# Token-major first stage with twelve places for modulation weights, and the gated branch sums on VectorE

## The reference

```
xs = x_sample + grid_pos_embed(rows)           # sin/cos of the row in channels 0:512, of the column in 512:1024
mod = silu(c) @ w_ada + b_ada                  # 6 x 1024 columns: shift1, scale1, gate1, shift2, scale2, gate2
h = rms_norm(x, g0) * (1 + scale1) + shift1
z = h @ w_in                                   # inputs of all mixers and the merge gates
y = (sig(gA) * A + sig(gB) * B + sig(gC) * C) @ w_out     # A Fourier, B pooling, C mLSTM, each projected
x = x + gate1 * rms_norm(y, g1)
x = x + gate2 * rms_norm(swiglu(rms_norm(x, g2) * (1 + scale2) + shift2), g3)
```

## Time and profile before

| | |
|---|---|
| median of three runs | 1853.43 us (1850.91 to 1862.03) |
| profiled execution | 1859.34 us |
| its span, first to last instruction | 1857.5 us |
| busy share TensorE / VectorE / ScalarE / GpSimd | 96 / 44 / 33 / 23% |
| transfers over the span | 296.19 MB, mean 159 GB/s |

### The profile page before, as it was taken

One profiled execution on the slowest core, in us unless ns is written; L12 is line 12 of the kernel. 1 busy time (PEld: TensorE's weight loads), 2 busy tenths in 40 slices (PEclk: granted clock), 3 DMA queues, 4 the chain that ended last, 5 costly groups with the idle time before them and its releaser, 6 DMA issues.

```text
span 1857.5 us, 24614 instructions
## 1 busy us (share of the span) xinstructions
PE 1783.0 (96%) x9794; PEld 1650.2 (89%) x9794; DVE 819.9 (44%) x1246; ACT 607.8 (33%) x1025; POOL 427.3 (23%) x481
## 2 busy tenths in 40 slices
PE   7799999999999999989989899999999999999997
PEld 4599998989999999988978799999999999888885
DVE  5500002241443434437768965444444443454543
ACT  2321112233222222223656482222222223343432
POOL 0300000323122233235335453222222210000000
PEclk9799999999999999999999999999999999999999
DMA  5544344665345566689768332222222226657572
GB/s 196 196 166 141 140 169 175 227 202 164 100 159 180 168 197 199 195 232 295 238 207 257 112 117 71 72 71 72 71 73 75 76 75 185 210 179 233 178 232 74
DMA packets 175386, 296.19 MB, mean 159 GB/s; under 512 B 11967, under 2 KB 122242, under 8 KB 175280
## 3 DMA queue, kind: packets, MB, share of 16 engines
q1 hardware_dynamic: 132016, 163.88, 27.4%
q0 software_dynamic: 27328, 90.73, 15.1%
q10 hardware_dynamic: 15936, 40.11, 6.4%
HBM read 231.57 MB, written 63.10 MB: 159 GB/s over the span
## 4 chain that ended last, share of the span: by engine, by line
PE 82%; DVE 7%; DMA 3%; ACT 3%; POOL 2%; issue 2%; ACTq 0%; DVEq 0%; SPq 0%; POOLq 0%
PE bank L532 25%; PE bank L534 25%; PE bank L533 25%; DVE w_lo L1652 2%; PE bank L722 1%; DMA mg<-z_scratch 1%; PE bank L751 1%; PE bank L954 1%; PE bank L957 1%; PE bank L964 1%; PE bank L972 1%; DMA raw<-in_w_ada 1%; POOL ya L2410 1%; DVE h_lo L2197 1%; DVE mg L1990 1%
## 5 line engine op out<-in xcount | busy, mean ns | idle before, releaser
L1652 DVE TENSOR_TENSOR w_lo<-raw,w_hi 128x1024 fp32r<-128x1024 f32 x218 | 283.8, 1304 | 377.7 <-ACT w_hi L1207 377.1
L532 PE MATMUL bank<-h_hi,w_hi 128*128 128x384 f32 x1080 | 377.2, 349 | 8.1 <-DVE h_lo L2197 5.5
L533 PE MATMUL bank<-h_lo,w_hi 128*128 128x384 f32 x1080 | 367.4, 340 | 0.0
L534 PE MATMUL bank<-h_hi,w_lo 128*128 128x384 f32 x1080 | 367.3, 340 | 0.0
L1207 ACT CAST w_hi<-raw 128x1024 fp32r<-128x1024 f32 x218 | 226.2, 1049 | 281.6 <-PE bank L534 174.2
L532 PEld LDWEIGHTS bank<-h_hi,w_hi 128*128 128x128 f32 x1080 | 205.5, 190 | 24.5 <-ACT z_st L1251 10.1
L533 PEld LDWEIGHTS bank<-h_lo,w_hi 128*128 128x128 f32 x1080 | 205.5, 190 | 0.1
L534 PEld LDWEIGHTS bank<-h_hi,w_lo 128*128 128x128 f32 x1080 | 205.1, 190 | 0.0
L534 PE MATMUL bank<-w_hi,f_lo 128*128 128x512 f32 x396 | 158.0, 399 | 0.0
L533 PE MATMUL bank<-w_lo,f_hi 128*128 128x512 f32 x396 | 156.0, 394 | 0.0
L532 PE MATMUL bank<-w_hi,f_hi 128*128 128x512 f32 x396 | 155.2, 392 | 0.0
(11 more groups left out here) (310 smaller groups left out, 3212.3 us busy)
## 6 DMA issues: line engine op xcount, KB each, us to landing
raw<-in_w_stream SPq DMA_DIRECT2D x209, 512.0 KB, 4.6
z_scratch<-z_st ACTq DMA_DIRECT2D x44, 576.0 KB, 3.1
raw<-in_w_ada SPq DMA_DIRECT2D x48, 512.0 KB, 5.1
mg<-z_scratch ACTq DMA_DIRECT2D x24, 576.0 KB, 6.8
f_raw<-f_scratch SPq DMA_DIRECT2D x66, 192.0 KB, 4.2
zt<-z_scratch POOLq DMA_DIRECT2D x27, 256.0 KB, 3.8
raw<-in_k_dft SPq DMA_DIRECT2D x9, 512.0 KB, 3.7
kv_scratch<-kv_st POOLq DMA_DIRECT2D x9, 512.0 KB, 4.5
```

The source lines that it names most:

```text
L532: pe.matmul(out, a_hi, b_hi, start=start, stop=False)
L533: pe.matmul(out, a_hi, b_lo, start=False, stop=False)
L534: return pe.matmul(out, a_lo, b_hi, start=False, stop=stop)
L1652: dve.tensor_tensor(w_lo[:, slot], raw[:, slot], w_hi[:, slot].bitcast(F32), ALU.subtract).then_inc(s_wlo, 1)
```

## The change

Start: the position is added to x token-major, in `x_in` itself. The row half comes from two rows of a table that TensorE spreads over 128 tokens (`spread_row`, one matmul with `sel`), the column half from a 128 x 512 table. ScalarE squares a tile of 1024 and sums it in the same instruction, takes the root; VectorE scales the tile into `xr`; TensorE turns `xr`, and ScalarE copies the banks to `xn`. `x_mean`, `xT`, `sq` and `rstd1` are gone. The sixteen first `w_ada` units have twelve places, four of `raw` and eight of `ada_raw`, which lies where `w_hi` and `w_lo` will be; the loads of units 12 to 15 wait for units 1, 2, 3 and 5, the others for no unit. TensorE multiplies units between the x tiles. The sum with the position is stored to DRAM (`xp_dram`) by GpSimd after `h_full`, and `x_load` reads it from there. Merge: the two additions into `ya` stand in VectorE's list, behind `y_low` of the chunk before; `pos_load` and `pos_add` are gone. Two loads of constants move behind the first four z units.

```diff
@@ SP, start
-                if n >= RAW:
-                    sp.wait_ge(s_unit, n - RAW + 1)
-                load(n % RAW, w_ada[n:n + 1])
-            sp.dma_start(cst[:, CB_EARLY:], k_cst[:, CB_EARLY:CB["pool"].start]).then_inc(s_const, 16)
-            sp.dma_start(cst_p[:], k_cst[:, CB["pool"].start:]).then_inc(s_const, 16)
+                place, landed, _ = ada_slot(n)
+                if RAW <= n < 3 * RAW:
+                    sp.wait_ge(s_xin[n - RAW], 16)
+                if n == ADA_FIRST - 1:
+                    sp.wait_ge(s_unit, RAW + 2)
+                elif n >= 3 * RAW:
+                    sp.wait_ge(s_unit, n - 3 * RAW + 2)
+                sp.dma_start(place, w_ada[n]).then_inc(landed, 16)
+                if n == ADA_FIRST - 3:
+                    sp.wait_ge(s_unit, 1)
+                    for half in range(2):
+                        r = slice(512 * half, 512 * half + 512)
+                        sp.dma_start(raw[:, 0, r], w_stream[0, :, r]).then_inc(s_raw[0], 16)
...
             z1_turn(0, True)
+            sp.dma_start(cst[:, CB_EARLY:], k_cst[:, CB_EARLY:CB["pool"].start]).then_inc(s_const, 16)
+            sp.dma_start(cst_p[:], k_cst[:, CB["pool"].start:]).then_inc(s_const, 16)
@@ TensorE, start
+            def spread_row(c):
...
+                pe.matmul(bank[7][:, :], sel[:].rearrange("r a w -> r (a w)"), pos_row[:, c, :], start=True,
+                          stop=True).then_inc(s_prow, 1)
             def start():
+                spread_row(0)
+                spread_row(1)
+                n = 0
                 for c in range(NT):
+                    if c + 2 < LAT // P:
+                        spread_row(c + 2)
                     x_tile(c)
                     if c == 4:
-                        x_mean(0)
-                    elif c == 7:
-                        x_mean(1)
-                pe.wait_ge(s_cpad, 1)
-                pe.wait_ge(s_early, 16)
-                for n in range(ADA_FIRST):
-                    blk = n // ADA_G
-                    ada_unit(n, n, n % ADA_G, blk % 2, blk - 1 if blk >= 2 else None)
-                    if n == 1:
-                        x_mean(2)
-                    if n % ADA_G == 1 and n > ADA_G:
-                        ada_turn(n // ADA_G - 1, (n // ADA_G - 1) % 2)
+                        pe.wait_ge(s_cpad, 1)
+                        pe.wait_ge(s_early, 16)
+                    for _ in range(2 if c >= 5 else int(c == 4)):
+                        ada_first(n)
+                        n += 1
+                for n in range(n, ADA_FIRST):
+                    ada_first(n)
                 ada_turn(ADA_FIRST // ADA_G - 1, 1)
@@ ScalarE, start
+                for c in range(NT):
...
+                    act.activation(x_sq[:], x_in[:, c], ACT.Square, accum_out=stat[:, c, 0:1]).then_inc(s_xsq, 1)
...
+                    act.activation(stat[:, c, 1:2], stat[:, c, 0:1], ACT.Sqrt, bias=eps[:, 0:1],
+                                   scale=1.0 / D).then_inc(s_xsq, 1)
+                    if c:
+                        x_out(c - 1)
+                x_out(NT - 1)
                 for blk in range(ADA_FIRST // ADA_G):
+                    if blk == ADA_FIRST // ADA_G - 1:
+                        split(ADA_FIRST, ADA_FIRST)
                     ada_out(blk, ADA_G * blk + ADA_G - 1)
@@ VectorE, start
+            def add_pos(c):
...
+                dve.tensor_tensor(x_in[:, c, 0:h], x_in[:, c, 0:h], bank[7][:, :], ALU.add).then_inc(s_padd, 1)
...
+                dve.tensor_tensor(x_in[:, c, h:D], x_in[:, c, h:D], pos_col[:], ALU.add).then_inc(s_padd, 1)
+            def x_norm(c):
...
+                dve.reciprocal(stat[:, c, 1:2], stat[:, c, 1:2]).then_inc(s_xrstd, 1)
...
+                dve.tensor_scalar(xr[:, c % 3], x_in[:, c], stat[:, c, 1:2], None, ALU.mult).then_inc(s_xr, 1)
             def start():
+                add_pos(0)
                 for c in range(NT):
+                    if c + 1 < LAT // P:
+                        add_pos(c + 1)
+                    x_norm(c)
+                split(ADA_FIRST, ADA_FIRST, 0)
+                dve.wait_ge(s_xn, 2 * NT)
                 modulation()
-                split(ADA_FIRST, ADA_FIRST, 0)
@@ VectorE, e1
                     if c:
                         y_low(x - 1)
+                    if x >= 2:
+                        dve.wait_ge(s_yl, x - 1)
+                    dve.wait_ge(s_ym, x + 1)
+                    dve.tensor_tensor(ya[:, x % 2], mg[x % MG][:, 0], mg[x % MG][:, 1], ALU.add).then_inc(s_ya, 1)
+                    dve.wait_ge(s_ya, 2 * x + 1)
+                    dve.tensor_tensor(ya[:, x % 2], ya[:, x % 2], mg[x % MG][:, 2], ALU.add).then_inc(s_ya, 1)
@@ GpSimd, after h_full
+            for c in range(NT):
+                pool.dma_start(xp_dram[c], x_in[:, c]).then_inc(s_xps, 16)
+            pool.wait_ge(s_xps, 16 * NT)
@@ GpSimd, e1 and e2
-                for c in range(KT):
...
-                    pool.tensor_tensor(ya[:, x % 2], mg[x % MG][:, 0], mg[x % MG][:, 1], ALU.add).then_inc(s_ya, 1)
...
-                    pool.tensor_tensor(ya[:, x % 2], ya[:, x % 2], mg[x % MG][:, 2], ALU.add).then_inc(s_ya, 1)
...
+                pool.dma_start(xt[:, m % 3], xp_dram[tile_at(position(m))]).then_inc(s_xl[m % 3], 16)
...
-                pos_load(3 * g)
-                for k in range(KT):
-                    if k in (2, 4, 6):
-                        m = 3 * g + k // 2 - 1
-                        pos_add(m)
-                        if k < 6:
-                            pos_load(m + 1)
-                    if g == NG - 1 and k == 2:
-                        combine(0)
+                if g == NG - 1:
+                    combine(0)
```

More of the change, by code:

```diff
@@ L98 @@
 FR = 6
+START_LOADS = (2, 3, 2, 2, 2, 2, 2, 2, 1)
 CHAIN = (1, 0, 2)
@@ L475, in kind_of @@
             return int(tile_at(q) == NT - 1)
-        def pos_adds(m):
-            return sum(not kind_of(position(i)) for i in range(m + 1))
         def product_done(j, i):
@@ L621, in z1_turn @@
                     n0 = ADA_FIRST + 3 * u
-                    sp.wait_ge(s_unit, i * 12 + (n0 - RAW + 1))
-                    load(n0 % RAW, w_stream[bass.ds(i * RAW + u, 1)])
+                    if not (first and u == 0):
+                        sp.wait_ge(s_unit, i * 12 + (n0 - RAW + 1))
+                        load(n0 % RAW, w_stream[bass.ds(i * RAW + u, 1)])
                     if first and u == 0:
@@ L714, in ada_unit @@
             def ada_unit(n, n0, part, b, before):
-                pe.wait_ge(s_raw[n0 % RAW], slot_count(n, n0))
+                if isinstance(n, int) and n < ADA_FIRST:
+                    src, landed, count = ada_slot(n)
+                    pe.wait_ge(landed, count)
+                else:
+                    src = raw[:, n0 % RAW]
+                    pe.wait_ge(s_raw[n0 % RAW], slot_count(n, n0))
                 if part == 0 and before is not None:
@@ L738, in x_tile, with ada_first @@
                 if c >= 2:
[L739 removed]
+                    pe.wait_ge(s_xn, 2 * (c - 1))
                 for k in range(KT):
[L741 removed]
+                    m = pe.transpose(bank[2 * u + k // 4][:, ktile(k % 4)], xr[:, c % 3, ktile(k)], ident)
                     if k % 4 == 3:
                         m.then_inc(s_xt, 1)
[L745 to L752 removed]
+            def ada_first(n):
+                blk = n // ADA_G
+                ada_unit(n, n, n % ADA_G, blk % 2, blk - 1 if blk >= 2 else None)
+                if n in (2 * ADA_G + 1, 2 * ADA_G + 2, 3 * ADA_G + 1):
+                    done = (2 * ADA_G + 1, 2 * ADA_G + 2, 3 * ADA_G + 1).index(n)
+                    ada_turn(done, done % 2)
@@ L1653, in split @@
                                   ALU.subtract).then_inc(s_wlo, 1)
-            def x_evac(c):
-                for half in range(2):
-                    dve.wait_ge(s_xt, 2 * c + half + 1)
-                    ps = bank[2 * (c % 2) + half][:, :].rearrange("p (k r w) -> p k r w", k=4, r=2)
-                    out = xT[:, 4 * half:4 * half + 4, c * P:(c + 1) * P].rearrange("p k (r w) -> p k r w", r=2)
-                    if half == 0:
-                        pos = last(K["pos_r"].rearrange("p (k r) -> p k r", k=4)[:, :, 2 * c:2 * c + 2], GRID_W)
-                    else:
-                        pos = K["pos_c"].rearrange("p (k w) -> p k w", k=4).unsqueeze(2).broadcast_to(
-                            (P, 4, 2, GRID_W))
-                    dve.tensor_tensor(out, ps, pos, ALU.add).then_inc(s_xev, 1)
             def gain(i):
```

165 lines of the change are left out of this document (70 added, 95 removed).

## The result

The changed kernel takes 1844.67 us (median of 7 runs, 1842.44 to 1849.04) against 1853.43 us: the ratio is 0.9948, with an interval of 0.993 to 0.9966. On a second chip it took 1842.62 us against 1855.62: 0.9929 (0.9911 to 0.9948). The gain is 9 to 13 us, not 28.5. The profiled execution of the changed kernel took 1845.1 us with a span of 1843.2, at its median; the one of the kernel before lay 6 us above its median, so the spans differ by more (14.3 us) than the medians.

The account below looks back on a forecast made before the run. The prediction took TensorE, busy 96% of the span, as the bound, with winnable idle time at the start and in the merge. Gains of 20 + 8.5 = 28.5 us from the median of 1853.43 gave 1825 us, range 1814 to 1840.

Parts of the forecast that it names:

- The bound and the places of the change: Whole kernel: TensorE, busy 96%, is the bound; time can be won at the start and in the merge.
- So ScalarE and VectorE share the pace at about 2.7 us a tile, TensorE needs 2.0 and is not the bound: Start, tile loop: pace of 2.7 us a tile, last root at 31.7 us; the start gives 20 us.
- sign of being wrong: Start, tile loop: the forecast is wrong if the loop takes over 3 us a tile.
- The rival of the low clock: New start: TensorE at 1.2 GHz doubles 7.5 + 1.0 us, adding 8.5 for 1834; chance 0.10.
- bound of about 41: Start, modulation weight transfers: even with a faster loop the end cannot come before about 41 us, bounding the gain at 25.
- `xt` is loaded from the scratch at the same place: Merge: reading `xt` from the scratch leaves its load where it was; no cost counted.
- merge's 8.5 us: Merge, `e1` and `e2`: sums on VectorE and no `pos_add` shrink TensorE's gaps, 8.5 us together.
- terms of the third `e1` and the last `e2`: Merge, late part: gains of 0.5 us in the third `e1` and 2.4 of 6.04 us in the last `e2`.
- The removed position loads and `pos_add` save TensorE nothing else: Merge: removing 8 x 512 KB of position loads and `pos_add` gives TensorE no further gain.
- The nine stores of x cost nothing: Second z unit's loads: stores of 9 x 512 KB, 11.5 us, fit in slack of 5 us; nothing counted.
- The merge gives nothing: Merge: VectorE in order, with ScalarE waits in its path, ends as late or 3 us later; 1833 to 1836, chance 0.11.
- The start gives half: Start: unit 8 onward still waits on a chain, so TensorE's gain halves; 1835, chance 0.05.

Follow-up runs that it names:

- pos_by_dma: Changed kernel with the row half of the position brought by a 128x512 transfer per tile instead of `spread_row` on TensorE; 1837.43 us, ratio 0.9893.
- four_places: Changed kernel with one more wait on SP that gives the sixteen modulation units their four places back; 1851.78 us, ratio 0.9985.
- late_pos: Changed kernel with the edits of late_loads and pos_by_dma together; 1833.63 us, ratio 0.9882.
- before_again: The kernel before, unaltered, run once more for a second trace; 1856.18 us, span 1854.4.
- after_again: The changed kernel, unaltered, run once more on the chip of its variants; 1842.62 us, ratio 0.9929.
- late_loads: Changed kernel with one more wait: GpSimd issues a group's x loads only when that group's sums are done; 1837.86 us, ratio 0.9901.
- adds_gpsimd: Changed kernel with the merge's sums back on GpSimd and the x loads behind them; 1840.54 us, ratio 0.9909.
- adds_pos: Changed kernel with sums back on GpSimd, x loads behind them, and the position's row half by transfer; 1836.57 us, ratio 0.9888.
- sums_late: Kernel before with the sums on VectorE, and GpSimd's x and position loads waiting for the group's sums; 1851.22 us, ratio 0.9971.
- sums_vector: Kernel before with only the merge's two sums per chunk moved from GpSimd to VectorE; 1860.47 us, ratio 1.0026.
- warm: Changed kernel with filler matmuls on TensorE: six before the first `spread_row`, two behind each of the first five tiles; 1836.18 us, ratio 0.9893.

## Why the prediction was wrong

**The bound and the places of the change: right.** Time was won at the start, and what was won there stayed won: 11.9 us at the first z matmul, and 11.0 at the place of the earlier trace rows (102.34 and 102.56 us before, 90.97 and 91.96 after), by the means of two traces each.

**"So ScalarE and VectorE share the pace at about 2.7 us a tile, TensorE needs 2.0 and is not the bound": the step that failed.** The rows used for it (5.43 us for `x_mean`, 1.07 for eight transposes) are those of full clock. In the changed kernel a tile is 2.07 + 1.97 us at the low clock less a small overlap, 3.9 us, back to back from 12.4 to 39 us. The first root was forecast at 11.3 and ended at 12.8 us; the last was forecast at 31.7 and ended at 42.5. That is 10.8 us late. That ScalarE comes next was right, with 2.33 us instead of 2.7: so much a tile takes where TensorE isn't in the way (pos_by_dma), and there the whole start gains 19 to 20 us, as forecast. The prediction's own sign of being wrong, a tile loop over 3 us, came true.

**The rival of the low clock was priced at the wrong place.** It was given 8.5 us, but for "7.5 + 1.0 us" of units and turns behind the tiles, and with a chance of 0.10, on the ground that "the tile loop leaves under 1 us". From 12.37 us on the loop left none at all, and the clock stayed low for 27 us of unbroken work. The units behind the tiles ran at full clock: from the start of the last tile's transposes (43.50 us) to the end of the last turn (55.5 us) it took 12.0 us, where the forecast had 13 (33.0 to 46.1). In the profile of before the sign was there: the first 40 transposes took 7.41 us, where five times 1.07 is 5.35. A single one took 421 ns until 9.8 us and 272 ns behind that, so the first part of them ran at the low clock, and I took the figure for full clock from a later row. So the start gave 12 and not 20. The time of that rival (1834) is still 11 us below the result, because the merge failed as well.

**The places carry most of the start: right.** four_places takes 9.2 us back. But the transfers were forecast without a break to about 38 us, and they rest from about 32 to 40 us (0 GB/s from 36 to 40, above): units 12 to 15 wait on SP for units 1, 2, 3 and 5, which were forecast for 27 to 32 us and of which unit 1 was multiplied only from 37.62 us on. It cost nothing here, since TensorE waited for none of them. In late_pos the weights do set the end: the last lands at 45.5 us. The prediction's bound of about 41 is not tested by that, as late_pos carries 2 MB more, 5 us at 409 GB/s.

**"`xt` is loaded from the scratch at the same place": wrong, and the merge's 8.5 us with it.** The code is at the same place, the time isn't. GpSimd's list is in order, and its sums had held the loads back. I gave no thought to what an engine does earlier when work is taken from it. That VectorE keeps up with TensorE's 4.27 us a chunk holds (it needs 3.93 us, 844.66 - 840.73, where nothing holds it up, and 4.2 were counted), `w_lo` at 1.22 holds, and "no gap above 1 us in the first `e1`" fails with a stop of 3.09 us behind a `raw` that landed late.

The terms can be told apart when the merge's stretch of the table is split at the matmul behind the stop of 2.55 us (937.34 us before, 928.00 in the changed kernel):

| kernel | up to there | from there |
|---|---|---|
| before, before_again | 106.0, 103.7 | 106.3, 106.1 |
| changed, after_again | 108.7, 109.3 | 102.5, 102.8 |
| late_loads, late_pos | 105.7, 105.4 | 102.4, 102.5 |
| adds_gpsimd, adds_pos | 104.4, 106.4 | 103.9, 104.1 |
| sums_late | 102.5 | 104.7 |

From there on 0.5 + 2.4 = 2.9 us were forecast and 3.6 came, 2.2 of them without the sums on VectorE (adds_gpsimd, adds_pos). So the terms of the third `e1` and the last `e2` hold together, although the last `e2` still stops for 5.23 us, where 6.04 - 2.4 = 3.6 was forecast; the `w_lo` in front of that stop takes 2.28 us beside `combine`, not 1.22. Up to there 3.2 + 2.4 = 5.6 us were forecast, and 4.2 were lost. The early loads are 3 to 4 of that (changed against late_loads), and 9 in sums_vector against sums_late (111.4 and 102.5). But with late loads this part still gave between a loss of 0.7 (late_loads, late_pos) and a gain of 2.3 (sums_late), so the two terms were too high besides; single traces scatter by 2 to 3 us here. One stop that was to go even grew: the one of 2.55 us is 3.12 to 3.14 us in all nine traces with the sums on VectorE, and 2.55 or 2.56 in the four with the sums on GpSimd. The prediction had named ScalarE's stalls there as something that would "now delay the sums as well"; that they are the cause is not shown.

**"The removed position loads and `pos_add` save TensorE nothing else": wrong by 1 to 2 us.** All kernels without them have 811.6 to 812.8 us in the last column, all kernels with them 813.8 or 813.9. One stop behind the last `e2` shrank from 2.82 to 1.17 us:

```profile
1063.81 0.41 PE L530 MATMUL bank<-T_hi,S_hi 128*128 128x384 f32 x1 [1.17 <-DVE S_lo L2084]
```

No run takes them out alone, so that they are the cause is argued from this split only.

**The nine stores of x cost nothing: right in the changed kernel.** ScalarE waits longer for a weight than before (10.63 us for the one at 88.36, where the earlier trace rows had 6.52), so the loads do come later beside the stores, but TensorE has no stop there: the 5 us of slack that the prediction found covered it. No run leaves the stores out, so that they are the reason for the longer wait is argued.

```profile
88.36 1.05 ACT L1242 CAST w_hi<-raw 128x1024 fp32r<-128x1024 f32 x1 [10.63 <-DMA raw<-in_w_stream]
```

**The other rivals.** "The merge gives nothing" came true in size, for a reason that it did not name (loads, not ScalarE in VectorE's way, are most of it). "The start gives half" came close in size, 12 of 20 us, also for another reason than it named. Each alone would have stayed in the range; together they left it, and I had not added them.

## What to carry to other kernels

Before a stage is costed with durations from a trace, look at which clock each row ran at, and cost the new stage at both; if the slower one makes TensorE the bound, that is the forecast until something shows that the clock is up by then. When work is taken from an engine that also issues transfers, list what stands behind that work in its queue: it will now start earlier, and a wait on the finished work of others keeps it where it was, as it did here at no price that these runs show. Test the parts of a change apart: here one part was worth 12 us, and the other lost 5 as made and won 5 with one more wait.

## What the runs showed of the hardware

- Until the level has risen for the first time, the granted-clock column cannot be trusted. It reads 1.00 in the tile loop from 16 to 36 us, while every TensorE operation there takes what it takes at 1.2 GHz: eight transposes 1.97 us, later 1.09 us, in one kernel. There the durations tell the level. In the traces where the level has been up once and falls again, column and durations agree: 0.50 in late_pos from 20 to 24 us, where eight transposes take 1.97 us, and 0.52 in warm from 12 to 16 us, behind a `spread_row` of 1.16 us at 8.65.
- Unbroken work did not bring the clock up at a fixed time. With the same code the first TensorE rows at full speed begin at 39.3 us (changed), at 41.5 (after_again) and at 34 (late_loads, adds_gpsimd), after TensorE had worked without a pause since 12 to 13 us in all of them. The first z matmul comes in the same order, between 55.9 and 59.0 us. With fillers of 128 rows the level was up from 18.7 us on to the end of the loop. In pos_by_dma, with no `spread_row`, it was up at about 28.7, although TensorE had paused for up to 0.98 us in a tile until then; in late_pos and adds_pos, with the same start, it was up for the eight transposes at 17.5 and 17.3 us (1.09 and 1.10 us), low again behind a pause of 1.25 us, and up from 26.4 and 30.0 us on. In every trace without fillers this last rise falls into a row of modulation units or to its start; whether they are the reason was not tried. What kept it low for so long under unbroken work stays open.
- Three loads of 512 KB issued beside the weight and `mg` loads raised the time of a 512 KB weight from issue to landing, but not from the 9.9 us of the kernel before to 17.6: the median over 40 us around the first `e1` is 9.0 to 9.9 us in the kernel before and in adds_gpsimd, 11.6 to 13.2 with the sums on VectorE and the x loads late (late_loads, late_pos, sums_late), and 17.6 to 17.8 in the changed kernel, after_again and four_places. So 4 to 6 us belong to the three loads. In the changed kernel (800 to 840 us):

```profile
raw<-in_w_stream SPq DMA_DIRECT2D x5, 512.0 KB, 17.6
...
xt<-xp_scratch POOLq DMA_DIRECT2D x3, 512.0 KB, 16.5
```
